# One phase for the set-up and the input of the state space block, its transposes spread between GEMM pieces, and attention logits that use both row halves

## Time and profile before

| | |
|---|---|
| median of 3 runs | 2651.75 us (2645.94 to 2652.28) |
| the profiled execution | 2651.7 us, of which the span of the trace is 2650.0 us |
| PE (matmul) busy | 2493.1 us, 94% of the span |
| POOL, DVE, ACT busy | 1495.9, 1012.4, 568.8 us |
| setup and mamba_in | 0 to 253.7 us |
| sb_attend | 1058.3 to 1183.0 us |

### The profile page before, as it was taken

How to read it: one execution, slowest core, us unless ns; L and a number is a source line. 1 busy time by engine, 2 the same in 40 slices (tenths; PEclk the granted TensorE clock), 3 DMA queues, 4 the chain that set the end, 5 groups by cost and what they waited for, 6 DMA issues and landing times.

```text
span 2650.0 us, 34683 instructions
## 1 busy us (share of the span) xinstructions
PE 2493.1 (94%) x14410; PEld 2023.6 (76%) x14410; DVE 1012.4 (38%) x1627; ACT 568.8 (21%) x1151; POOL 1495.9 (56%) x1396
## 2 busy tenths in 40 slices
PE   8998998999999999999999999998578998999998
PEld 6777886788888887558888877666477787888887
DVE  3443848064042400335503335775542332421023
ACT  1112323012011011761201102345433210110010
POOL 7544555568487486336858746461121664666663
PEclk9997999999999999999999998999788999999999
DMA  5212022223233133002323313130000322333321
GB/s 169 80 50 72 1 79 81 88 96 104 80 111 95 64 120 97 7 16 96 104 88 104 96 58 94 35 104 17 1 3 3 92 88 79 102 98 95 95 80 64
DMA packets 104289, 199.06 MB, mean 75 GB/s; under 512 B 9306, under 2 KB 12612, under 8 KB 104132
## 3 DMA queue, kind: packets, MB, share of 16 engines
q1 hardware_dynamic: 101476, 189.36, 23.4%
q10 hardware_dynamic: 2656, 7.47, 0.8%
HBM read 194.71 MB, written 2.10 MB: 74 GB/s over the span
## 4 chain that ended last, share of the span: by engine, by line
PE 84%; DVE 9%; ACT 2%; POOL 2%; issue 2%; DMA 0%; POOLq 0%; DVEq 0%; SPq 0%; ACTq 0%
PE psum L153 35%; PE psum L293 23%; PE psum L155 8%; PE psum L232 3%; PE psum L1253 1%; POOL weight_split_ring L412 1%; PE psum L968 1%; PE psum L194 1%; PE psum L1262 1%; DVE big L873 1%; PE psum L982 1%; PE psum L1281 1%; DVE big L1821 1%; PE psum L2102 1%; PE psum L2126 1%
## 5 line engine op out<-in xcount | busy, mean ns | idle before, releaser
L412 POOL TENSOR_TENSOR weight_split_ring<-weight_ring,weight_split_ring 128x512 fp32r<-128x512 f32 (+2 forms) x732 | 953.7, 1323 | 30.6
L153 PE MATMUL psum<-x_split,weight_split_ring 128*128 128x512 f32 x4080 | 958.5, 394 | 2.0 <-POOL weight_split_ring L412 1.3
L153 PEld LDWEIGHTS psum<-x_split,weight_split_ring 128*128 128x128 f32 x4080 | 767.0, 189 | 171.9 <-issue 11.6
L409 POOL TENSOR_SCALAR weight_split_ring<-weight_ring 128x1024 fp32r<-128x1024 f32 (+2 forms) x366 | 395.1, 1080 | 734.3 <-PE psum L293 340.3
L293 PE MATMUL psum<-weight_split_ring,hidden_split 128*128 128x512 f32 x2448 | 576.2, 396 | 8.2 <-DVEq L2929 8.2
L293 PEld LDWEIGHTS psum<-weight_split_ring,hidden_split 128*128 128x128 f32 x2448 | 460.1, 188 | 119.9 <-DVEq L2929 8.6
L155 PE MATMUL psum<-weight_split_ring,x_split 128*128 128x512 f32 (+2 forms) x1056 | 240.5, 388 | 2.0 <-DVEq L2929 1.4
L155 PEld LDWEIGHTS psum<-weight_split_ring,x_split 128*128 128x128 f32 x1056 | 197.0, 207 | 44.4 <-issue 7.2
L708 DVE TENSOR_TENSOR big<-big 128x512 f32<-128x512 f32 x64 | 88.7, 1386 | 179.6 <-ACT big L693 179.6
L511 DVE SCALAR_TENSOR_TENSOR residual<-residual,psum 128x512 f32<-128x512 f32 x48 | 32.8, 683 | 261.8 <-PE psum L293 261.8
L693 ACT ACTIVATE big<-psum 128x512 f32<-128x512 f32 x64 | 38.3, 598 | 434.9 <-PE psum L153 378.8
(11 more groups left out here) (329 smaller groups left out, 2517.6 us busy)
## 6 DMA issues: line engine op xcount, KB each, us to landing
weight_ring<-in_mlp_w SPq DMA_DIRECT2D x128, 512.0 KB, 3.7
weight_ring<-in_w_in SPq DMA_DIRECT2D x92, 512.0 KB, 3.6
weight_ring<-in_w_ffn_in SPq DMA_DIRECT2D x40, 512.0 KB, 3.6
weight_ring<-in_w_out SPq DMA_DIRECT2D x24, 512.0 KB, 3.8
weight_ring<-in_w_ffn_out SPq DMA_DIRECT2D x22, 512.0 KB, 3.7
weight_ring<-in_sb_w_q SPq DMA_DIRECT2D x8, 512.0 KB, 3.8
weight_ring<-in_sb_w_k SPq DMA_DIRECT2D x8, 512.0 KB, 3.7
weight_ring<-in_sb_w_v SPq DMA_DIRECT2D x8, 512.0 KB, 3.7
```

The source lines that it names most:

```text
L153: mm = pe.matmul(out, wp[:, k, m * P:(m + 1) * P], xp, start=first, stop=last)
L409: pool.tensor_scalar(part.high[:, 0:nk, 0:n], raw, 1.0, 0.0, ALU.mult, ALU.add).then_inc(self.high_made, 1)
L412: low = pool.tensor_tensor(part.low[:, k, 0:n], raw[:, k, :], part.high[:, k, 0:n].bitcast(F32), ALU.subtract)
```

## The change

**Setup and mamba_in become one phase.** The weights are read in the order x columns 0 to 511 (`g0`, tiles 0 to 3), the 32 time-step columns (`gd`), the remaining 3584 columns (`g1`, 7 parts, tiles 4 to 31). PE turns x, runs half of `g0`, turns the parameter rows, runs the other half, runs `gd`, then the parts j = 0 to 6 of `g1`. Before piece 5 of part 0 it sums the decays. Tile 4j + i is transposed ahead of piece `at[i]` of part j, where `at` is 9, 11, 13, 15 for part 0 and 4, 7, 10, 13 afterwards. ACT does silu 0 to 3, the time steps, and then turned(n - 4), silu(n) for n from 4. DVE does conv 0 to 3, the time steps, conv 4 to 31. POOL splits 6 chunks, cuts the constants, and goes on.

**Attention logits.** q and k of heads 2 and up (without the first 128 tokens) are also copied by DMA into the other row half, two DMAs for each pair of heads on ACT's queue. From head 2 on the logits of blocks 1 to 3 read the copy, those of block 0 the original.

```diff
+        pe.wait_ge(s_sel, 1)
+        for n in range(2 * NT):
+            turn_x(n)
+        pe.wait_ge(s_xl, 2 * NT)
+        go_on(first, 8)
+        turn_parameters()
+        go_on(first, 8)
+        go_on(small, ROUNDS)
+        for j in range(len(g1.parts)):
+            at = [9, 11, 13, 15] if j == 0 else [4, 7, 10, 13]
+            for r in range(ROUNDS):
+                if j == 0 and r == 5:
+                    decay_sums()
+                if r in at and 4 * j + at.index(r) < TURNED:
+                    turn(4 * j + at.index(r))
+                go_on(wide, 1)
...
+        def turn(n):
+            pe.wait_ge(s_silu, n + 1)
+            if n < 2:
+                pe.wait_ge(s_exp, SUMS_READ)
+                pe.wait_ge(s_dt, TO_END)
+            else:
+                pe.wait_ge(s_tf, n - 1)
...
+    def scalar(act):
...
+        for n in range(NT):
+            silu(n)
+        time_steps()
+        for n in range(NT, XBC_TILES + NT):
+            if n - NT < TURNED:
+                turned(n - NT)
+            if n < XBC_TILES:
+                silu(n)
...
+                    if n == 0:
+                        pe.wait_ge(s_sw[(h // 2) % 2], 32 * ((h // 2 + 1) // 2))
                 for b in blocks:
-                    mm = pe.matmul(bank(h, b), m.kF[rows(h), h // 2, b * P:(b + 1) * P], m.qF[rows(h), h // 2, b * P:],
-                                   start=(b != 3), stop=True, skip_group_check=True)
+                    if h >= 2 and b >= 1:
+                        k, q = other_k(h, b), other_q(h, b)
+                    else:
+                        k, q = m.kF[rows(h), h // 2, b * P:(b + 1) * P], m.qF[rows(h), h // 2, b * P:]
+                    mm = pe.matmul(bank(h, b), k, q, start=(b != 3), stop=True, skip_group_check=True)
...
+        def copy_halves(p):
+            if p >= 3:
+                act.wait_ge(s_z, NS * (2 * p - 2))
+            for g in range(2):
+                act.dma_start(m.swap[rows(g + 1), p % 2], m.qkF[rows(g), :, p, P:]).then_inc(s_sw[p % 2], 16)
...
+        copy_halves(1)
+        copy_halves(2)
         ln(0)
         for h in range(SB_HEADS + 2):
             if h + 1 < SB_HEADS:
                 ln(h + 1)
+            if h % 2 == 0 and 2 <= h <= SB_HEADS - 6:
+                copy_halves(h // 2 + 2)
```

More of the change, by code:

```diff
@@ L731, in load_parameters, with more_constants, mamba_in @@
         sp.dma_start(m.head_rows[:, n, :], ap.partition_broadcast(P)).then_inc(m.parameter_rows_landed, 16)
-def setup(nc, kit, m, a):
+CONSTANT_STEPS = 7
+def more_constants(kit, m, pool):
+    cut = Chain(pool, m.constants_cut)
+    for t, sign, b in ((m.upper, 1, 0), (m.upper_strict, 1, -1), (m.neg_lower, -1, 0)):
+        cut.mark(pool.affine_select(out=t[:, :], in_=t[:, :], compare_op=ALU.is_ge, fill=0.0, base=b,
+                                    pattern=[[sign, P]], channel_multiplier=-sign))
+    cut(pool.tensor_scalar(m.ident_r, m.ident, 1.0, 0.0, ALU.mult, ALU.add))
+    cut(pool.tensor_scalar(m.past_r, m.upper, -FAR, FAR, ALU.mult, ALU.add))
+    cut(pool.memset(m.halves[0:64, 0:64], 1.0))
+    cut(pool.memset(m.halves[64:P, 64:P], 1.0))
+    assert cut.n == CONSTANT_STEPS
+def mamba_in(nc, kit, m, a):
+    BK = 6
+    w_in = a["w_in"]
+    g0 = Gemm(kit, w_in, KD, D_INNER, WIDE, True, banks=BK)
+    gd = Gemm(kit, w_in, KD, D_INNER + XBC, SSM_HEADS, False, banks=BK)
+    g1 = Gemm(kit, w_in, KD, D_INNER + WIDE, XBC - WIDE, True, banks=BK)
+    TURNED = X_TILES + SSM_GROUPS
+    ROUNDS = 16
     s_base = kit.sem("constant_filled")
@@ new lines, in mamba_in, with tile, gemm, x_block @@
+    ABS, DA, TO_END = 1, 2, 3
+    SUMS_READ, WEIGHT = 4, 5
+    PARAMETERS, SUMS = 2 * NT + 1, 2 * NT + 2
+    LANDED = 16 * (len(ROWS) + 4)
+    nrow = sum(n for _, n in ROWS)
+    def tile(n):
+        return m.xring[:, n % 8, :] if n < X_TILES else m.bcF[:, n - X_TILES, :]
+    def gemm(n):
+        return (g0, n) if n < NT else (g1, n - NT)
+    def x_block(n):
+        t, j = n // 2, n % 2
+        return t, slice(4 * j, 4 * j + 4), slice(t * P, (t + 1) * P)
+    def tensor(pe):
+        first, small, wide = (g.stream(pe, m.x_tile) for g in (g0, gd, g1))
+        def go_on(stream, n):
+            for _ in range(n):
+                next(stream)
+        def turn_x(n):
+            t, feats, _ = x_block(n)
+            if n % 2 == 0:
+                pe.wait_ge(m.x_landed[t], 16)
+            if n >= 4:
+                pe.wait_ge(s_xl, n - 3)
+            for q in range(4):
+                f = feats.start + q
+                mm = pe.transpose(kit.psum[:, n % 4, q * P:(q + 1) * P], m.h[:, t, f * P:(f + 1) * P], m.ident[:, :])
+            mm.then_inc(s_xt, 1)
+        def turn_parameters():
+            pe.wait_ge(s_par, LANDED)
+            pe.transpose(kit.psum[:, 7, 0:nrow], m.par_rows[0:nrow, 0, :], m.ident[0:nrow, 0:nrow])
+            pe.transpose(kit.psum[:, 7, P:2 * P], m.par_rows[:, 1, :], m.ident[:, :]).then_inc(s_xt, 1)
+        def decay_sums():
+            pe.wait_ge(s_dt, DA)
+            pe.wait_ge(s_xh, PARAMETERS)
+            pe.wait_ge(m.constants_cut, CONSTANT_STEPS)
+            for c in range(NT):
+                pe.matmul(kit.psum[:, 6, c * 32:c * 32 + 32], m.upper[:, :], m.da[:, c, :], start=True, stop=True)
+                mm = pe.matmul(kit.psum[:, 7, c * 32:c * 32 + 32], m.ones[:, :], m.da[:, c, :], start=True, stop=True)
+            mm.then_inc(s_xt, 1)
+        def turn(n):
[5 more added lines that the diff above has]
+                pe.wait_ge(s_tf, n - 1)
+            for c in range(NT):
+                mm = pe.transpose(kit.psum[:, BK + n % 2, c * P:(c + 1) * P], tile(n)[:, c * P:(c + 1) * P],
+                                  m.ident[:, :])
+            mm.then_inc(s_tr, 1)
+        pe.wait_ge(s_sel, 1)
[14 more added lines that the diff above has]
+                go_on(wide, 1)
@@ new lines, in scalar, with silu, turned, time_steps @@
+    def scalar(act):
+        def silu(n):
+            g, i = gemm(n)
+            g.wait_free(act, i)
+            act.activation(tile(n), tile(n), ACT.Silu).then_inc(s_silu, 1)
+        def turned(n):
+            act.wait_ge(s_tr, n + 1)
+            f = n if n < X_TILES else n - X_TILES
+            dst = (m.xT_tok if n < X_TILES else m.bTok)[:, :, f * P:(f + 1) * P]
+            act.activation(dst, kit.psum[:, BK + n % 2, :].rearrange("p (c d) -> p c d", c=NT), ACT.Copy).then_inc(s_tf, 1)
+        def time_steps():
+            act.wait_ge(s_par, LANDED)
+            act.activation(m.head_rows[:, 1, :], m.head_rows[:, 1, :], ACT.Exp).then_inc(s_exp, 1)
+            act.wait_ge(s_dt, ABS)
+            act.activation(m.dt_abs[:, :, :], m.dt_abs[:, :, :], ACT.Exp, scale=-1.0).then_inc(s_exp, 1)
+            act.wait_ge(s_exp, 2)
+            act.activation(m.dt_abs[:, :, :], m.dt_abs[:, :, :], ACT.Ln, bias=m.one).then_inc(s_exp, 1)
+            act.wait_ge(s_xt, SUMS)
+            cs, end = kit.psum[:, 6, 0:P], kit.psum[:, 7, 0:P]
+            act.activation(m.ncs[:, :, :].rearrange("p a b -> p (a b)"), cs, ACT.Copy, scale=-1.0)
+            act.activation(m.ecs[:, :, :].rearrange("p a b -> p (a b)"), cs, ACT.Exp)
+            act.activation(m.eend[:, :, :].rearrange("p a b -> p (a b)"), end, ACT.Exp).then_inc(s_exp, 1)
+            act.wait_ge(s_dt, TO_END)
+            act.activation(m.wend[:, :, :], m.wend[:, :, :], ACT.Exp).then_inc(s_exp, 1)
+        for n in range(2 * NT):
+            _, feats, cols = x_block(n)
+            act.wait_ge(s_xt, n + 1)
+            act.activation(m.xin.high[:, feats, cols], kit.psum[:, n % 4, :].rearrange("p (q c) -> p q c", q=4),
+                           ACT.Copy).then_inc(s_xh, 1)
+        act.wait_ge(s_xt, PARAMETERS)
+        act.activation(m.par_cols[:, 0, 0:nrow], kit.psum[:, 7, 0:nrow], ACT.Copy)
+        act.activation(m.par_cols[:, 1, :], kit.psum[:, 7, P:2 * P], ACT.Copy).then_inc(s_xh, 1)
+        for n in range(NT):
+            silu(n)
+        time_steps()
+        for n in range(NT, XBC_TILES + NT):
[3 more added lines that the diff above has]
+                silu(n)
@@ L755, in gpsimd @@
         cut.wait()
[L756 to L795, removed]
-CONSTANT_STEPS = 7
-def more_constants(kit, m, pool):
-    cut = Chain(pool, m.constants_cut)
-    for t, sign, b in ((m.upper, 1, 0), (m.upper_strict, 1, -1), (m.neg_lower, -1, 0)):
-        cut.mark(pool.affine_select(out=t[:, :], in_=t[:, :], compare_op=ALU.is_ge, fill=0.0, base=b,
-                                    pattern=[[sign, P]], channel_multiplier=-sign))
-    cut(pool.tensor_scalar(m.ident_r, m.ident, 1.0, 0.0, ALU.mult, ALU.add))
-    cut(pool.tensor_scalar(m.past_r, m.upper, -FAR, FAR, ALU.mult, ALU.add))
-    cut(pool.memset(m.halves[0:64, 0:64], 1.0))
-    cut(pool.memset(m.halves[64:P, 64:P], 1.0))
-    assert cut.n == CONSTANT_STEPS
@@ L815, in mamba_in @@
-def mamba_in(nc, kit, m, a):
-    BK = 6
[L819 to L831, removed]
-    def tile(n):
```

(19 more changed lines are left out.)

60 lines of the change are left out of this document (54 added, 6 removed).

## The result

The changed kernel takes 2657.3 us (median of 8 runs, 2655.09 to 2659.5) against 2646.12 us for the kernel before (8 runs, 2642.05 to 2652.48): a ratio of 1.0036, 95% interval 1.0023 to 1.0049. Slower by about 9.5 us (6 to 13 by the interval), where +9.3 had been forecast. The medians themselves differ by 11.2 us: the kernel before ran at 2642 in some executions and at 2652 in others. The span of its profiled execution is 2657.1 us, 7.1 over that of before.

The account below looks back on a forecast made before the run. PE was taken as the bound (busy 94%), alternating with ACT in attention. Terms -3.3 + 2.1 + 11.4 + 6.2 - 7.1 = +9.3 us on 2651.7 gave 2661 us, own range 2655 to 2668, 8 in 10 range 2654 to 2669.

Parts of the forecast that it names:

- The start: Start of mamba_in: without the phase end PE's GEMM begins earlier, -3.7, parameter transposes +0.4; -3.3 us, bounds -3.6 to -3.0.
- The time steps: mamba_in: 11.5 us before the scan goes; decay sums 2.5, half-clock restart 1.9, bare end 9.1 come; +2.1 us.
- The restart: mamba_in: 512-column matmuls restart at half clock after the small ones; 1.9 us lost, from 1.6 to 2.3.
- The tail: End of mamba_in: convolutions of the last four tiles and the last silu run bare, the scan waits; 9.1 us.
- The turns: mamba_in: PE's fourth turn waits for ACT's copy queued behind a late silu, 4.66 us in parts 1 to 5; +11.4 us.
- Breaking the stream: mamba_in: price of interrupting PE's stream of matmuls 24 times with turns; 0.3 us.
- The clock: mamba_in: PE's clock falls in the stops, 10.7 us against 4.5 before; +6.2 us, bounds +3.5 to +9.
- Rival (D): mamba_in: the clock stays up in the 4.66 us stops, so not slower; 2650 us, 7%.
- The logits: Attention: block 0 runs beside block 1 in the other row half, 7 pairs x 1.01; -7.1 us, bounds 0 to -9.
- Rival (A): Attention: row halves don't overlap in this order, or ACT gives it back; 2668 us, 8%.
- Rival (B): Attention: program order holds, each head gains only 0.32 us, -4.5 instead of -7.1; 2664 us, 10%.
- Rival (C): Attention: the copies' DMA issues hold ACT, 5 pairs x 0.8 = +4; 2665 us, 6%.

Follow-up runs that it names:

- e3: The changed kernel with each copy of a turned tile one place ahead in ScalarE's order, before the silu; 2622.51 us, 0.9903 of the kernel before.
- e4: The changed kernel with the fourth turn of parts 1 to 5 ahead of piece 15 instead of 13; 2635.1 us, 0.9944 of the kernel before.
- e6: The changed kernel with the fourth turn of parts 1 to 5 ahead of piece 14 instead of 13; 2648.79 us (one run).
- e1: The kernel before with the attention edit alone (copies into the other row half, logits of blocks 1 to 3 from them); 2642.86 us, 0.9978 of before.
- e7: The changed kernel with the copies still made but all logits read from the original; 2659.61 us (one run).

## Why the prediction was right, step by step

**The start.** -4.1 us instead of -3.7, since the first chunk was split by 13.7, not 14.2; the parameter turns cost 0.13, not 0.4. The clock gave 0.7 of it back: the first 96 matmuls, two stretches of 48, lost 2.9 us, not 2.2. `g0` ended at 38.8 us, and the steps of the prediction (first chunk, clock, 96 matmuls, parameter turns) give 14.2 + 2.2 + 21.9 + 0.4 = 38.7.

**The time steps.** The small GEMM took 16.9 us (38.79 to 55.69), not 18.2, the sums 1.7 us (65.01 to 66.71), not 2.5. The restart lost 9.48 - 0.17 - 30 x 0.228 = 2.5 us, not 1.9. The tail was 258.64 to 267.90, 9.26 us, against 9.1. Together about 1.3 us better than forecast.

**The turns.** The stops of parts 1 to 5 were 4.65 us against 4.66 forecast, 5 of 5, with the cause as stated; e3 removes them by their cause, e4 and e6 shorten them by the pieces put ahead. Breaking the stream was priced too low: 18 matmuls between two turns take 4.19 us from start to start (95.55 to the turn at 99.74), where 18 x 0.228 is 4.10, and 24 such breaks make some 2 us, not 0.3. In part 0 the stop was 1.48 us, not 2.8, and this step was wrong: I had put a table load behind the late convolution. The timeline of ACT shows it done long before, right after the first copy, which leaves 2.8 - 1.28 = 1.5:

```profile
73.53 1.28 ACT L914 ACT_TABLE_LOAD   x1
82.06 0.63 ACT L914 ACTIVATE big<-big 128x512 f32<-128x512 f32 x1 [7.24 <-DVE big L875]
```

**The clock.** Forecast 10.7 us lost behind the stops. Measured: the five stretches (10.91, 11.38, 11.73, 11.79 us for 42 matmuls, 28.11 for 114) are 8.8 us over their full-clock length, and four of the turns took 0.36 more each: 10.2 us. That e3 gained 35.0 us at the scan's start, 24.7 of them stops, gives 10.3. Rival (D) falls; its deciding point, 2.7 us of idle time, was too low as a rule, as e6 and the late fall at 108.6 show.

**The logits.** Forecast -7.1, measured -5.5 by the pairs and -5.8 by e1. The mechanism held, a size was off: the head in which PE is the bound gained 0.43 us, not 0.64. Block 0's first pass starts 0.12 us behind block 1's, and its second 0.53 us later, where 512 columns take 0.43 alone (half of block 0's 0.85). The ACT-bound head gained 0.35 (1102.94 to 1108.77 is 5.83 us against 6.18), of the 0.37 forecast. Rival (A) falls by e1. Rival (B) has a size near the measured one, 0.32 against 0.43 and 0.35, but its order is not what the records show: block 0's first pass started 0.21 us ahead of block 1's second. That answers the Trainium skill's sentence, page "TensorE: Matmul & The Clock Gate", section "Part 3: Packing small matmuls", that matmuls start strictly in program order; for matmuls of different row halves these records say otherwise. The first two heads, which the change leaves alone, show it for whole matmuls, in narrow windows of the trace of before:

```profile
1061.04 1.10 PE L1253 MATMUL psum<-big 64*128 64x128 f32 x3
1061.09 1.06 PE L1253 MATMUL psum<-big 64*128 64x512 f32 x2
```

The record of 128 columns that starts at 1061.04 is of head 1, as head 0's two started at 1059.38 and 1059.60; the one of 512 columns that starts at 1061.09 is of head 0 and stands before it in the program. Rival (C) falls by e7: 0.1 us a pair, 0.7 us in all, where it had 4.

**The sum.** At the scan's start +14.2 against a forecast of +16.4; the table load (1.3 us) and the time steps (1.3 us) take off 2.6 us, the clock 0.4 more, and the dearer breaks put part of it back. The attention phase gave -5.5 against -7.1. The two misses have opposite signs: the terms measured make +8.7, the forecast's made +9.3. That the ratio's +9.5 lies 0.2 us from the forecast is therefore luck; its interval runs from 6 to 13 us, and the sum hides a miss of 2.2 in one phase and of 1.6 in the other. Between single traces, places that the change doesn't touch differ too: from the scan's start to the attention phase the changed kernel is 2.7 us shorter, for the gate's 384 matmuls alone 90.02 us in the trace of before and 87.33 in that of the changed kernel, since more of the former ran at half clock. A scatter of this size is enough to set the spans (+7.1) and the ratio (+9.5) apart. The forecast of 2661 us in all started from a median of 2651.7 us of 3 runs; the 8 runs' median is 5.6 us lower, and so the changed kernel came out at 2657.3.
